# Hybrid decoder layer: order of the down projection's loads, and of splits and small tiles where two stages meet

## The chip, the cores and the metric

The kernel runs on one core of a Trainium2 chip. The metric is the device time in microseconds (us) of one execution, lower is better. Other times below come from one profiled execution, whose own clock starts at zero.

## The reference, cut to what matters

One layer (model width 2048, 512 tokens, all fp32): a token mixer, a cross-attention, a SwiGLU channel mixer and a last norm. The change lies in the channel mixer:

```python
D_FF = -(-8 * D_MODEL // (3 * 256)) * 256        # 5632

def swiglu(h, w_gate_up, w_down):
    gu = h @ w_gate_up
    g, u = gu[..., :D_FF], gu[..., D_FF:]
    return (jax.nn.silu(g) * u) @ w_down

    ...
    h = h + swiglu(rms_norm(h, g_ffn[l]), w_gate_up[l], w_down[l])
return rms_norm(h, g_final)
```

## The kernel before

Every fp32 operand is split into a high part, which ScalarE (ACT) writes by copying into the rounded type, and a low part, the difference, which VectorE (DVE) writes. Each product is then three matmuls: high·high, low·high, high·low. So before TensorE (PE) may use a piece of weights, a load must land, ACT must write the high part (`hi`, L894, or L1181 in the blocks), and DVE the low part (`lo`, L1284, or L1734 in the blocks). Four semaphores carry this: a raw buffer is loaded, high ready, low ready, used.

The hidden width 5632 is 44 tiles of 128. **Tiles 0 to 3** are computed by plain products (line group G_U0 is the last of them). DVE's `first_hidden` (L1725, L1727: two operations a tile) scales and multiplies them out of four banks, ACT's `hidden_hi` (L1151) and DVE's `hidden_lo` (L1708) split each tile, and GpSimd's queue (POOL) spills it to DRAM (L505).

**Tiles 4 to 43** are the 40 blocks. A block computes a gate and an up tile by a Strassen-like scheme of seven products named P1, Q5, P2, P6, P7, P4, P3, each of two halves of 12 matmuls with 256 columns (L835 to L837). `cycle_products` gives the order: P1 and Q5 of block 0 first, then for each block b: P2, P6, P1 of b+1, P7, Q5 of b+1, P4, P3. Some weights are sums of loaded pieces; DVE makes them in place (`sum_x1` to `sum_x4`, L1742 to L1761, 128x1024). The splits go into eight slots, in turn. ACT takes snapshots of a bank between products (`copy_p1` L1190, `copy_p1_p6` L1197, `copy_p1_p6_p7` L1204) and does the silu (L1210); DVE takes the outputs out: `gate_first`, `gate_second` (L1777), `up_second`, `up_first` (L1790), `up_scaled` (L1796), `hidden_out` (L1802).

**The down stage** multiplies all 44 hidden tiles, read back from DRAM, with `w_down`: eight column groups, hh = 0, 1 (hidden tiles 0 to 21 and 22 to 43) by c = 0 to 3 (512 output columns), each of 22 steps k. A step is 12 matmuls with 512 columns (L524 to L526), with k's 128 rows of weights in one of four slots (`w_hi`, `w_lo`). The raw weights come in loads of 256 rows, p = 0 to 10 for a column group, into the four raw buffers; a load may be issued once the low parts of the load four before it are written. The hidden tiles are loaded by `hidden_load(h)` into places in SBUF that the blocks leave: 0 to 11 into `s_res`, each four once a product is done, 12 to 27 into `h_both`, 28 and 29 into `s_res`, all of these 18 once the last block is done. The residual comes back from DRAM in four parts into `acc`, which needs the last spill to have landed, as they share SBUF. Column group c adds onto part c.

What sets the order is written by hand: each engine runs its instructions strictly as written, and a wait holds up all that stands behind it. SyncE's queue (SP) issues all the loads. Before, SP issues the first four raw loads of the down stage (L462), then all 30 hidden tiles (L454), then the four parts of the residual (L468), and then the other raw loads (L381). ACT and DVE finish the last block's silu, up and hidden output and then split the first four steps of weights.

Of the kernel before, what the change touches and what calls it, by code (L numbers as in the profile page):

```python
# [46 lines left out]
HT = FF // P  # L47
HH = HT // 2
# [24 lines left out]
B_DOWN = B_U0 + KT  # L73
# [16 lines left out]
SPL = 4  # L90
# [13 lines left out]

def cycle_products(b):

    more = b + 1 < BLOCKS
    return [("P2", b), ("P6", b)] + [("P1", b + 1)] * more + [("P7", b)] + [("Q5", b + 1)] * more + [("P4", b), ("P3", b)]


def product_counts():
# [14 lines left out]
def build(nc, x, mem, g_mix, w_in, conv_w, sinks, w_attn_o, w_conv_o, w_out, g_xattn, g_mem,  # L126
          w_xq, w_xkv, w_xo, g_ffn, w_gate_up, w_down, g_final, rope, out):
    with ExitStack() as ctx:
# [235 lines left out]
        def _(sp):  # L364
# [91 lines left out]
            def down_load(hh, c, p):  # L456

                load((B_DOWN + HH * (4 * hh + c)) // 2, 0, None, p, wd, hh * HH * P + 256 * p, 512 * c)

            for p in range(RAW):  # L460
                sp.wait_ge(s_blo, NUMBER["P7" if p == 1 else "P3" if p == 3 else "P4", BLOCKS - 2] + 2)
                sp.dma_start(raw[:, p, :, :], wd[256 * p:256 * p + 256, 0:512].rearrange("(b p) n -> p b n", p=P)).then_inc(s_raw[p], 16)  # L462
            for h in range(len(PLACES)):
                hidden_load(h)
            for i in range(2):
                sp.wait_ge(s_hsp[i], 16 * (HT // 2))
            for c in range(4):
                sp.dma_start(acc[:, 4 * c:4 * c + 4, :], acc_dram[c]).then_inc(s_ald[c], 16)  # L468
            for hh in range(2):
                for c in range(4):  # L470
                    for p in range(HH // 2):
                        if hh or c or p >= RAW:
                            down_load(hh, c, p)
                        if hh and c == 0 and 2 * p + len(PLACES) < HT:
                            hidden_load(len(PLACES) + 2 * p)
                            hidden_load(len(PLACES) + 2 * p + 1)
# [403 lines left out]
        def _(act):  # L880
            def hi(b0, g, k, gain=None, per=0, gper=0, i=None):

                n = (b0 + k) // 2
                s = (b0 + k) % SPL
                if k % 2 == 0:
                    act.wait_ge(s_raw[n % RAW], 16 * (n // RAW + 1) + (i * (2 * per) if i is not None else 0))

                if k == SPL - 1 and g:
                    act.wait_ge(s_done, 4 * g + (i * (4 * gper) if i is not None else 0))
                elif b0 + k >= SPL:  # L890
                    before = g if k >= SPL else g - 1
                    act.wait_ge(s_used, b0 + k - SPL + 1 - before + (i * (per - gper) if i is not None else 0))
                sc = 1.0 if gain is None else gain[:, k:k + 1]
                nc.scalar.activation(w_hi[:, s, :], raw[:, n % RAW, (b0 + k) % 2, :], ACT.Copy, scale=sc).then_inc(s_hi, 1)  # L894
# [251 lines left out]
            def hidden_hi(h):  # L1146

                act.wait_ge(s_upp, h + 1)
                if h >= 2:
                    act.wait_ge(s_hsp[h % 2], 16 * (h // 2))  # L1150
                nc.scalar.activation(hid_t[:, h % 2, 0, :], up_t[:, h % 2, :], ACT.Copy).then_inc(s_ahi, 1)  # L1151
# [31 lines left out]
            def copy_p1(b):  # L1183

                act.wait_ge(s_bused, NUMBER["P1", b] + 2)
                if b >= 2:
                    act.wait_ge(s_g1, b - 1)
                elif b == 1:
                    act.wait_ge(s_upp, 4)
                nc.scalar.activation(snap[b % 2][SNAP_A], reg_a[b % 2][:, 0:TH], ACT.Copy).then_inc(s_ca, 1)  # L1190
# [15 lines left out]
            def silu(b):  # L1206

                act.wait_ge(s_g1n, b + 1)
                act.wait_ge(s_g2, b + 1)
                nc.scalar.activation(gate_t[:, b % 2, :], gate_t[:, b % 2, :], ACT.Silu).then_inc(s_silu, 1)  # L1210

            block_hi("P1", 0)
            block_hi("Q5", 0)
            hidden_hi(0)
            hidden_hi(1)
            copy_p1(0)
            for b in range(BLOCKS):
                for name, n in cycle_products(b):
                    block_hi(name, n)
                    if name == "P2" and b == 0:  # L1220
                        hidden_hi(2)
                        hidden_hi(3)
                    if name == "P6" and b:
                        silu(b - 1)
                    if name == "P7":
                        copy_p1_p6(b)
                        if b:
                            hidden_hi(3 + b)
                    if name == "P4":
                        copy_p1_p6_p7(b)  # L1230
                        if b + 1 < BLOCKS:
                            copy_p1(b + 1)
            silu(BLOCKS - 1)
            for k in range(SPL):
                act.wait_ge(s_bused, HALVES - SLOTS + k + 1 if (HALVES + k) % SLOTS < SPL else HALVES)
                hi(B_DOWN, G_DOWN, k)
            hidden_hi(HT - 1)
            for k in range(SPL, HH):
                hi(B_DOWN, G_DOWN, k)
# [18 lines left out]
        def _(dve):  # L1258
# [446 lines left out]
            def hidden_lo(h):  # L1705

                dve.wait_ge(s_ahi, h + 1)
                nc.vector.tensor_tensor(hid_t[:, h % 2, 1, :], up_t[:, h % 2, :], hid_t[:, h % 2, 0, :], ALU.subtract).then_inc(s_alo, 1)  # L1708
# [10 lines left out]
            def first_hidden(j):  # L1719

                done(G_U0, j)
                dve.wait_ge(s_gate, 32 + j + 1)
                if j >= 2:
                    dve.wait_ge(s_alo, j - 1)
                nc.vector.tensor_tensor(up_t[:, j % 2, :], banks(G_U0)[j][:, :], rbc[:, :], ALU.mult).then_inc(s_freed, 1)  # L1725
                dve.wait_ge(s_freed, 4 * G_U0 + j + 1)
                nc.vector.tensor_tensor(up_t[:, j % 2, :], up_t[:, j % 2, :], tile4[:, j, :], ALU.mult).then_inc(s_upp, 1)  # L1727
# [9 lines left out]
            def sum_x1(b):  # L1737

                dve.wait_ge(s_braw[b % 2][1], 16 * (b // 2 + 1))
                dve.wait_ge(s_blo, NUMBER["P1", b] + 2)  # L1740
                w = braw[b % 2]
                nc.vector.tensor_tensor(w[:, 0, :, :], w[:, 0, :, :], w[:, 1, :, :], ALU.add).then_inc(s_x1, 1)  # L1742
# [8 lines left out]
            def sum_x3(b):  # L1751

                dve.wait_ge(s_x1, b + 1)
                w = braw[b % 2]
                nc.vector.tensor_tensor(w[:, 1, :, :], w[:, 1, :, :], w[:, 3, :, :], ALU.add).then_inc(s_x3, 1)
# [36 lines left out]
            def up_scaled(b):  # L1792

                dve.wait_ge(s_u1, b + 1)
                dve.wait_ge(s_u2, b + 1)
                nc.vector.tensor_tensor(up_t[:, b % 2, :], up_t[:, b % 2, :], rbc[:, :], ALU.mult).then_inc(s_un, 1)  # L1796

            def hidden_out(b):

                dve.wait_ge(s_silu, b + 1)  # L1800
                dve.wait_ge(s_un, b + 1)
                nc.vector.tensor_tensor(up_t[:, b % 2, :], up_t[:, b % 2, :], gate_t[:, b % 2, :], ALU.mult).then_inc(s_upp, 1)  # L1802
# [2 lines left out]
            sum_x1(0)  # L1805
            block_lo("Q5", 0)
            sum_x2(0)
            first_hidden(0)
            first_hidden(1)
            hidden_lo(0)  # L1810
            first_hidden(2)
            hidden_lo(1)
            first_hidden(3)
            for b in range(BLOCKS):
                for name, n in cycle_products(b):
                    block_lo(name, n)
                    if name == "P2":
                        sum_x3(b)
                        if b:
                            gate_second(b - 1)  # L1820
                        else:
                            hidden_lo(2)
                            hidden_lo(3)
                    if name == "P6":
                        if b:
                            up_first(b - 1)
                        sum_x4(b)
                        if b:
                            up_scaled(b - 1)
                    if name == "P1":  # L1830
                        if b:
                            hidden_out(b - 1)
                        sum_x1(n)
                    if name == "P7":
                        if b + 1 == BLOCKS:
                            hidden_out(b - 1)
                        gate_first(b)
                        if b:
                            hidden_lo(3 + b)
                    if name == "Q5":  # L1840
                        sum_x2(n)
                    if name == "P4":
                        up_second(b)
            gate_second(BLOCKS - 1)
            up_first(BLOCKS - 1)
            up_scaled(BLOCKS - 1)
            hidden_out(BLOCKS - 1)
            for k in range(SPL):
                lo(B_DOWN, 0, None, k)
            hidden_lo(HT - 1)  # L1850
            for k in range(SPL, HH):
                lo(B_DOWN, 0, None, k)
# [69 lines left out]
```

## Time and profile before

| what | value |
|---|---|
| time, median of 3 runs | 2753.96 us (2753.07 to 2754.15) |
| the profiled execution | 2752.59 us, of which span 2750.8 us |
| PE / DVE / ACT busy | 98% / 58% / 39% of the span |
| mean granted clock of PE | 0.992 |
| PE, longest waits | 20.0 us and 3.0 us (L524), 4.7 us (L835) |

PE is a pipeline: a row's time from start to end is longer than the distance to the next start, so the pace is read from the starts: 0.12 us for 256 columns and 0.227 us for 512 at full clock. At half clock they are 0.21 and 0.43. The profile's rows give the idle time of an engine ahead of a row in square brackets, and who ended it. SPq rows are the issue of loads, not their transfer.

### The profile page before, as it was taken

How to read it: one execution, taken by the hardware profiler on the slowest of the kernel's cores; microseconds unless marked ns; L12 is line 12 of the kernel's file. 1: busy time of each engine (PE TensorE's matmuls, PEld its weight loads, DVE VectorE, ACT ScalarE, POOL GpSimd, SP SyncE). 2: the span in 40 equal slices, each digit the busy share in tenths (PEclk: the TensorE clock that was granted, in tenths of full speed). 3: DMA queues.
4: the chain of work that ended last, by engine and by line, in shares of the span. 5: the costliest groups of instructions: out<-in, count | busy, mean ns of one | idle time of the engine just before them, and what ended most of it. 6: DMA issues, size and time to landing. Idle time of an engine off the chain costs nothing.

```text
span 2750.8 us, 39364 instructions
## 1 busy us (share of the span) xinstructions
PE 2702.6 (98%) x15433; PEld 2385.9 (87%) x15433; DVE 1587.9 (58%) x2791; ACT 1071.5 (39%) x1996; POOL 28.8 (1%) x60
## 2 busy tenths in 40 slices
PE   8999999999999999999999999999999969999998
PEld 7888888888888888887889999999999968888887
DVE  4557775333333445457778888888888833222334
ACT  4334543323232333345644444444444422222221
POOL 0000000000000000000000000000000000000000
PEclk9999999999999999999999999999999989999999
DMA  5332222333333333333444434444344493235232
GB/s 165 96 92 77 77 75 87 100 93 98 99 92 99 97 111 113 95 114 121 138 138 126 143 116 139 131 131 139 116 144 126 123 369 113 94 121 183 93 99 92
DMA packets 277058, 328.40 MB, mean 119 GB/s; under 512 B 10444, under 2 KB 174372, under 8 KB 274980
## 3 DMA queue, kind: packets, MB, share of 16 engines
q1 hardware_dynamic: 269572, 295.82, 35.2%
q0 software_dynamic: 7328, 30.41, 2.7%
q8 instruction: 106, 1.74, 0.3%
q14 instruction: 52, 0.43, 0.0%
HBM read 294.74 MB, written 31.46 MB: 119 GB/s over the span
## 4 chain that ended last, share of the span: by engine, by line
PE 95%; DVE 2%; SPq 1%; DMA 1%; issue 0%; ACT 0%; DVEq 0%
PE bank L524 19%; PE bank L525 19%; PE bank L526 19%; PE bank L835 10%; PE bank L837 10%; PE bank L836 10%; PE bank L539 2%; PE bank L541 2%; PE bank L540 2%; SPq L454 1%; DMA raw<-in_w_down_dram 1%; PE bank L646 1%; PE bank L632 0%; DVE y_out L1897 0%; DVE h_lo L1309 0%
## 5 line engine op out<-in xcount | busy, mean ns | idle before, releaser
L1284 DVE TENSOR_TENSOR w_lo<-raw,w_hi 128x512 fp32r<-128x512 f32 x352 | 243.2, 692 | 564.8 <-ACT w_hi L894 563.8
L894 ACT ACTIVATE w_hi<-raw 128x512 fp32r<-128x512 f32 x352 | 221.8, 631 | 647.8 <-PE bank L526 616.8
L1286 DVE SCALAR_TENSOR_TENSOR w_lo<-raw,par,w_hi 128x512 fp32r<-128x512 f32 x320 | 239.9, 751 | 394.6 <-ACT w_hi L894 393.7
L524 PE MATMUL bank<-h_hi,w_hi 128*128 128x512 f32 x1088 | 428.0, 393 | 0.0
L526 PE MATMUL bank<-h_hi,w_lo 128*128 128x512 f32 x1088 | 423.8, 390 | 0.0
L525 PE MATMUL bank<-h_lo,w_hi 128*128 128x512 f32 x1088 | 423.8, 390 | 0.0
L894 ACT ACTIVATE w_hi<-raw,par 128x512 fp32r<-128x512 f32 x320 | 231.3, 724 | 467.0 <-PE bank L526 380.8
L526 PEld LDWEIGHTS bank<-h_hi,w_lo 128*128 128x128 f32 x1088 | 204.2, 188 | 43.5
L524 PEld LDWEIGHTS bank<-h_hi,w_hi 128*128 128x128 f32 x1088 | 204.4, 188 | 40.3 <-issue 0.2
L525 PEld LDWEIGHTS bank<-h_lo,w_hi 128*128 128x128 f32 x1088 | 204.5, 188 | 40.0
L1734 DVE TENSOR_TENSOR w_lo<-braw,w_hi 128x512 fp32r<-128x512 f32 x280 | 179.7, 686 | 13.8 <-ACT w_hi L1181 13.8
L524 PE MATMUL bank<-s_res,w_hi 128*128 128x512 f32 x416 | 163.6, 393 | 23.0 <-DVE w_lo L1284 23.0
L835 PE MATMUL bank<-s_hi,w_hi 128*128 128x256 f32 x648 | 183.5, 283 | 0.5 <-ACT snap L1197 0.5
L1734 DVE TENSOR_TENSOR h_lo<-braw,h_hi 128x512 fp32r<-128x512 f32 x280 | 179.5, 686 | 7.5 <-ACT h_hi L1181 7.4
L836 PE MATMUL bank<-s_lo,w_hi 128*128 128x256 f32 x648 | 183.4, 283 | 0.0
L837 PE MATMUL bank<-s_hi,w_lo 128*128 128x256 f32 x648 | 183.4, 283 | 0.0
L835 PE MATMUL bank<-s_hi,h_hi 128*128 128x256 f32 x632 | 178.9, 283 | 0.0
L836 PE MATMUL bank<-s_lo,h_hi 128*128 128x256 f32 x632 | 178.8, 283 | 0.0
L837 PE MATMUL bank<-s_hi,h_lo 128*128 128x256 f32 x632 | 178.8, 283 | 0.0
L525 PE MATMUL bank<-s_res,w_hi 128*128 128x512 f32 x416 | 163.1, 392 | 0.0
L526 PE MATMUL bank<-s_res,w_lo 128*128 128x512 f32 x416 | 163.0, 392 | 0.0
L1181 ACT ACTIVATE w_hi<-braw 128x512 fp32r<-128x512 f32 x280 | 158.3, 624 | 11.5 <-PE bank L526 6.2
(259 smaller groups left out, 5989.0 us busy)
## 6 DMA issues: line engine op xcount, KB each, us to landing
braw<-in_w_gate_up_dram SPq DMA_DIRECT2D x160, 512.0 KB, 4.7
raw<-in_w_in_dram SPq DMA_DIRECT2D x136, 512.0 KB, 3.7
raw<-in_w_down_dram SPq DMA_DIRECT2D x88, 512.0 KB, 3.7
hidden_spilled<-hid_t POOLq DMA_DIRECT2D x44, 512.0 KB, 3.6
raw<-in_w_out_dram SPq DMA_DIRECT2D x32, 512.0 KB, 3.6
s_res<-hidden_spilled SPq DMA_DIRECT2D x26, 512.0 KB, 7.5
h_both<-hidden_spilled SPq DMA_DIRECT2D x18, 512.0 KB, 11.6
raw<-in_w_conv_o_dram SPq DMA_DIRECT2D x16, 512.0 KB, 3.7
```

The lines of the kernel that those rows point to most:

```text
L524: pe.matmul(o_, w_hi[:, s, c], hi, start=(k == 0), stop=False)
L525: pe.matmul(o_, w_hi[:, s, c], lo, start=False, stop=False)
L526: mm = pe.matmul(o_, w_lo[:, s, c], hi, start=False, stop=(k == n - 1))
L539: pe.matmul(bk[j][:, :], hi[:, c], w_hi[:, s, :], start=(k == 0), stop=False)
L835: pe.matmul(r[:, 0:TH], w_h[:, q, :], u_h, start=(not on and half == 0 and q == 0), stop=False, skip_group_check=on)
L836: pe.matmul(r[:, 0:TH], w_h[:, q, :], u_l, start=False, stop=False, skip_group_check=on)
L837: mm = pe.matmul(r[:, 0:TH], w_l[:, q, :], u_h, start=False, stop=(half == 1 and q == 3), skip_group_check=on)
L894: nc.scalar.activation(w_hi[:, s, :], raw[:, n % RAW, (b0 + k) % 2, :], ACT.Copy, scale=sc).then_inc(s_hi, 1)
L1181: nc.scalar.activation(slot_hi[n % SLOTS], weights(name, b)[:, 4 * half:4 * half + 4, :], ACT.Copy).then_inc(s_bhi, 1)
L1284: nc.vector.tensor_tensor(w_lo[:, s, :], src, w_hi[:, s, :], ALU.subtract).then_inc(s_lo, 1)
L1286: nc.vector.scalar_tensor_tensor(w_lo[:, s, :], src, g[:, k:k + 1], w_hi[:, s, :], ALU.mult, ALU.subtract).then_inc(s_lo, 1)
L1734: nc.vector.tensor_tensor(slot_lo[n % SLOTS], weights(name, b)[:, 4 * half:4 * half + 4, :], slot_hi[n % SLOTS], ALU.subtract).then_inc(s_ ...
```

## The change

`cycle_products` is written in another way with the same result. The rest is order.

```diff
@@ SP, the down stage @@
-            for h in range(len(PLACES)):
+            for h in range(12):
                 hidden_load(h)
-            for i in range(2):
-                sp.wait_ge(s_hsp[i], 16 * (HT // 2))
-            for c in range(4):
-                sp.dma_start(acc[:, 4 * c:4 * c + 4, :], acc_dram[c]).then_inc(s_ald[c], 16)
             for hh in range(2):
                 for c in range(4):
                     for p in range(HH // 2):
+                        if hh == 0 and c == 0 and 4 <= p < 9:
+                            hidden_load(2 * p + 4)
+                            hidden_load(2 * p + 5)
                         if hh or c or p >= RAW:
                             down_load(hh, c, p)
+                        if hh == 0 and 1 <= c < 3 and p < 4:
+                            hidden_load(HH + 4 * (c - 1) + p)
+                        if hh == 0 and p == 9:
+                            if c == 0:
+                                for i in range(2):
+                                    sp.wait_ge(s_hsp[i], 16 * (HT // 2))
+                            sp.dma_start(acc[:, 4 * c:4 * c + 4, :], acc_dram[c]).then_inc(s_ald[c], 16)
@@ ACT @@
             block_hi("P1", 0)
             block_hi("Q5", 0)
-            hidden_hi(0)
-            hidden_hi(1)
-            copy_p1(0)
             for b in range(BLOCKS):
                 for name, n in cycle_products(b):
                     block_hi(name, n)
                     if name == "P2" and b == 0:
-                        hidden_hi(2)
-                        hidden_hi(3)
-                    if name == "P6" and b:
-                        silu(b - 1)
+                        copy_p1(0)
+                    if name == "P6":
+                        if b:
+                            silu(b - 1)
+                        else:
+                            hidden_hi(0)
+                            hidden_hi(1)
                     if name == "P7":
                         copy_p1_p6(b)
-                        if b:
-                            hidden_hi(3 + b)
+                        hidden_hi(3 + b if b else 2)
+                    if name == "Q5" and b == 0:
+                        hidden_hi(3)
...
+            for k in range(SPL):
+                act.wait_ge(s_bused, HALVES - SLOTS + k + 1)
+                hi(B_DOWN, G_DOWN, k)
             silu(BLOCKS - 1)
-            for k in range(SPL):
-                act.wait_ge(s_bused, HALVES - SLOTS + k + 1 if (HALVES + k) % SLOTS < SPL else HALVES)
-                hi(B_DOWN, G_DOWN, k)
             hidden_hi(HT - 1)
@@ DVE @@
             sum_x2(0)
-            first_hidden(0)
-            first_hidden(1)
-            hidden_lo(0)
-            first_hidden(2)
-            hidden_lo(1)
-            first_hidden(3)
...
+            for k in range(SPL):
+                lo(B_DOWN, 0, None, k)
             gate_second(BLOCKS - 1)
             up_first(BLOCKS - 1)
             up_scaled(BLOCKS - 1)
             hidden_out(BLOCKS - 1)
-            for k in range(SPL):
-                lo(B_DOWN, 0, None, k)
             hidden_lo(HT - 1)
```

Inside DVE's loop over the blocks, `first_hidden` and `hidden_lo` of tiles 0 to 3 now stand among the first products: behind P2's splits and `sum_x3` tiles 0 and 1; behind P6's and `sum_x4` the low part of tile 0, tile 2, the low part of tile 1; behind P1's tile 3; behind Q5's the low part of tile 2; and in block 1, behind P2's, the low part of tile 3.

**First place: DVE, between the weight sums of block 0.** Names: `braw0` and `braw1` hold raw weights of even and odd blocks, `h_lo` and `w_lo` as outputs are low parts of a half product, `up_t` with `bank` and then with `tile4` are the two operations of `first_hidden`, `hid_t` is `hidden_lo`. Before:

```order
1220 L1749 TENSOR_TENSOR braw0_93<-braw0_93 128x1024
1221 L1725 TENSOR_TENSOR up_t_96<-bank0,rbc_103 128x512
1222 L1727 TENSOR_TENSOR up_t_96<-up_t_96,tile4_100 128x512
...
1229 L1725 TENSOR_TENSOR up_t_96<-bank3,rbc_103 128x512
1230 L1727 TENSOR_TENSOR up_t_96<-up_t_96,tile4_100 128x512
1231 L1734 TENSOR_TENSOR h_lo_50<-braw0_93,h_hi_49 128x4x128 x2
1232 L1755 TENSOR_TENSOR braw0_93<-braw0_93 128x1024
1233 L1708 TENSOR_TENSOR hid_t_97<-up_t_96,hid_t_97 128x512 x2
1234 L1734 TENSOR_TENSOR h_lo_50<-braw0_93,h_hi_49 128x4x128 x2
```

The four tiles and two low parts stood ahead of P2's low parts. In the changed kernel, the same engine and place:

```order
1220 L1757 TENSOR_TENSOR braw0_93<-braw0_93 128x1024
1221 L1742 TENSOR_TENSOR h_lo_50<-braw0_93,h_hi_49 128x4x128 x2
1222 L1763 TENSOR_TENSOR braw0_93<-braw0_93 128x1024
1223 L1733 TENSOR_TENSOR up_t_96<-bank0,rbc_103 128x512
...
1227 L1742 TENSOR_TENSOR h_lo_50<-braw0_93,h_hi_49 128x4x128 x2
1228 L1769 TENSOR_TENSOR braw0_93<-braw0_93 128x1024
1229 L1716 TENSOR_TENSOR hid_t_97<-up_t_96,hid_t_97 128x512
1230 L1733 TENSOR_TENSOR up_t_96<-bank2,rbc_103 128x512
...
1233 L1742 TENSOR_TENSOR w_lo_53<-braw1_94,w_hi_52 128x512 x2
1234 L1733 TENSOR_TENSOR up_t_96<-bank3,rbc_103 128x512
```

P2's two low parts now come right behind the sum, and the tiles are spread behind the splits of P2, P6 and P1.

**Second place: DVE, from the last block to the down stage.** `w_lo` out of `raw` is a low part of down weights. Before:

```order
1983 L1777 TENSOR_TENSOR gate_t_95<-bank7,rbc_103 128x256
1984 L1790 TENSOR_TENSOR up_t_96<-bank0,snap1_102 128x256
1985 L1796 TENSOR_TENSOR up_t_96<-up_t_96,rbc_103 128x512
1986 L1802 TENSOR_TENSOR up_t_96<-up_t_96,gate_t_95 128x512
1987 L1284 TENSOR_TENSOR w_lo_53<-raw_51,w_hi_52 128x512 x4
1988 L1708 TENSOR_TENSOR hid_t_97<-up_t_96,hid_t_97 128x512
```

The four low parts closed the row. In the changed kernel they stand ahead of the gate's second half:

```order
1984 L1292 TENSOR_TENSOR w_lo_53<-raw_51,w_hi_52 128x512 x4
1985 L1785 TENSOR_TENSOR gate_t_95<-bank7,rbc_103 128x256
1986 L1798 TENSOR_TENSOR up_t_96<-bank0,snap1_102 128x256
1987 L1804 TENSOR_TENSOR up_t_96<-up_t_96,rbc_103 128x512
1988 L1810 TENSOR_TENSOR up_t_96<-up_t_96,gate_t_95 128x512
1989 L1716 TENSOR_TENSOR hid_t_97<-up_t_96,hid_t_97 128x512
```

ACT's four high parts move in the same way, ahead of the last silu.

**Third place: SP, from the last block into the down stage.** Before:

```order
178 L454 DMA s_res<-hidden_spilled 128x1024 x12
179 L454 DMA h_both<-hidden_spilled 128x2x512 x16
180 L454 DMA s_res<-hidden_spilled 128x1024 x2
181 L468 DMA acc<-residual_spilled 128x2048 x4
182 L381 DMA raw<-in_w_down_dram 128x2x512 x41
```

In the changed kernel:

```order
178 L455 DMA s_res<-hidden_spilled 128x1024 x12
179 L455 DMA h_both<-hidden_spilled 128x2x512 x2
180 L382 DMA raw<-in_w_down_dram 128x2x512
181 L455 DMA h_both<-hidden_spilled 128x2x512 x2
182 L382 DMA raw<-in_w_down_dram 128x2x512
183 L455 DMA h_both<-hidden_spilled 128x2x512 x2
184 L382 DMA raw<-in_w_down_dram 128x2x512
...
188 L382 DMA raw<-in_w_down_dram 128x2x512 x2
189 L480 DMA acc<-residual_spilled 128x2048
190 L382 DMA raw<-in_w_down_dram 128x2x512 x2
191 L455 DMA h_both<-hidden_spilled 128x2x512
```

Eighteen hidden tiles and four parts of the residual stood ahead of the fifth raw load; now two hidden tiles do, and the rest goes between later raw loads.

## Rows read from the trace of the kernel before

**Rows 1.** Page, busy time by engine (first line), and PE's waits: total, times, longest.
```profile
PE 2702.6 (98%) x15433; PEld 2385.9 (87%) x15433; DVE 1587.9 (58%) x2791; ACT 1071.5 (39%) x1996; POOL 28.8 (1%) x60
...
PE bank L524 <- DVE w_lo L1284: 23.0, 2, 20.0
PE bank L835 <- DVE h_lo L1734: 4.7, 1, 4.7
```

**Rows 2.** Timeline of PE around the long wait: start, us, engine, line, operation, count, [idle].
```profile
2250.60 0.39 PE L526 MATMUL bank<-s_res,w_lo 128*128 128x512 f32 x1
2271.00 0.79 PE L524 MATMUL bank<-s_res,w_hi 128*128 128x512 f32 x1 [20.01 <-DVE w_lo L1284]
...
2275.00 0.43 PE L524 MATMUL bank<-s_res,w_hi 128*128 128x512 f32 x1
```

**Rows 3.** Timeline of SP's queue and of ACT, from the last block into the down stage.
```profile
2203.03 17.44 SPq L454 DMA_DIRECT2D s_res<-hidden_spilled  x12
2224.51 20.98 SPq L454 DMA_DIRECT2D h_both<-hidden_spilled  x16
...
2247.44 3.11 SPq L468 DMA_DIRECT2D acc<-residual_spilled  x4
2250.60 46.14 SPq L381 DMA_DIRECT2D raw<-in_w_down_dram  x10
...
2269.59 1.15 ACT L894 ACTIVATE w_hi<-raw 128x512 fp32r<-128x512 f32 x2 [28.81 <-DMA raw<-in_w_down_dram]
```

**Rows 4.** Raw loads of line L381, 2200 to 2300 us: issue to landing.
```profile
DMA to landing us min/median/max: 3.6/4.4/19.7
```

**Rows 5.** Stretches: length, busy PE, PEld, DVE, ACT, POOL, clock granted, DMA share, GB/s.
```profile
2214.00:2218.00 4.00, 3.52 (x28) 3.11 (x26) 1.90 (x3) 1.95 (x4) 0.53 (x1) 1.00 0.66 223
2226.00:2228.00 2.00, 0.57 (x2) 0.51 (x3) 2.00 (x4) 0.63 (x1) 0.00 (x0) 0.82 1.02 420
2228.00:2230.00 2.00, 2.00 (x6) 1.62 (x5) 1.47 (x3) 0.00 (x0) 0.23 (x1) 0.50 1.02 398
2240.00:2250.00 10.00, 10.00 (x46) 8.29 (x45) 0.69 (x1) 0.63 (x1) 0.00 (x0) 1.00 1.05 387
```

**Rows 6.** Timeline of PE where the blocks end and the down stage begins.
```profile
2224.20 0.28 PE L837 MATMUL bank<-s_hi,h_lo 128*128 128x256 f32 x1
2227.43 0.77 PE L524 MATMUL bank<-s_res,w_hi 128*128 128x512 f32 x1 [2.95 <-DVE w_lo L1284]
...
2230.86 0.39 PE L526 MATMUL bank<-s_res,w_lo 128*128 128x512 f32 x1
```

**Rows 7.** Timeline of DVE and ACT there.
```profile
2224.51 0.42 DVE L1790 TENSOR_TENSOR up_t<-bank,snap 128x256 f32<-128x256 f32 x1 [2.45 <-PE bank L837]
2226.38 2.49 DVE L1284 TENSOR_TENSOR w_lo<-raw,w_hi 128x512 fp32r<-128x512 f32 x4
...
2218.31 1.14 ACT L1181 ACTIVATE h_hi<-braw 128x512 fp32r<-128x512 f32 x2
2222.70 2.17 ACT L894 ACTIVATE w_hi<-raw 128x512 fp32r<-128x512 f32 x4
```

**Rows 8.** Timeline of PE at the first block.
```profile
1409.24 0.28 PE L835 MATMUL bank<-h_hi,w_hi 128*128 128x256 f32 x1
...
1419.84 0.55 PE L835 MATMUL bank<-h_hi 128*128 128x256 f32 x1 [4.68 <-DVE h_lo L1734]
...
1425.10 0.31 PE L835 MATMUL bank<-s_hi,h_hi 128*128 128x256 f32 x1
```

**Rows 9.** Timeline of DVE at the first block.
```profile
1410.90 1.22 DVE L1749 TENSOR_TENSOR braw<-braw 128x1024 f32<-128x1024 f32 x1
1412.04 0.68 DVE L1725 TENSOR_TENSOR up_t<-bank,rbc 128x512 f32<-128x512 f32 x1
...
1413.37 0.68 DVE L1725 TENSOR_TENSOR up_t<-bank,rbc 128x512 f32<-128x512 f32 x1
...
1419.01 1.28 DVE L1734 TENSOR_TENSOR h_lo<-braw,h_hi 128x512 fp32r<-128x512 f32 x2
1420.21 1.22 DVE L1755 TENSOR_TENSOR braw<-braw 128x1024 f32<-128x1024 f32 x1
...
1434.36 0.42 DVE L1783 TENSOR_TENSOR up_t<-bank,mask 128x256 f32<-128x256 f32 x1 [0.99 <-ACT mask L1204]
```

More of the change, by code:

```diff
@@ L105, in cycle_products @@
 def cycle_products(b):
-    more = b + 1 < BLOCKS
-    return [("P2", b), ("P6", b)] + [("P1", b + 1)] * more + [("P7", b)] + [("Q5", b + 1)] * more + [("P4", b), ("P3", b)]
+    if b + 1 == BLOCKS:
+        return [("P2", b), ("P6", b), ("P7", b), ("P4", b), ("P3", b)]
+    return [("P2", b), ("P6", b), ("P1", b + 1), ("P7", b), ("Q5", b + 1), ("P4", b), ("P3", b)]
 def product_counts():
@@ L1818, in _ @@
                         sum_x3(b)
+                        if b == 0:
+                            first_hidden(0)
+                            first_hidden(1)
+                        elif b == 1:
+                            hidden_lo(3)
                         if b:
                             gate_second(b - 1)
-                        else:
-                            hidden_lo(2)
-                            hidden_lo(3)
                     if name == "P6":
@@ L1829, in _ @@
                             up_scaled(b - 1)
+                        else:
+                            hidden_lo(0)
+                            first_hidden(2)
+                            hidden_lo(1)
                     if name == "P1":
@@ L1832, in _ @@
                             hidden_out(b - 1)
+                        else:
+                            first_hidden(3)
                         sum_x1(n)
@@ L1841, in _ @@
                         sum_x2(n)
+                        if b == 0:
+                            hidden_lo(2)
                     if name == "P4":
                         up_second(b)
+            for k in range(SPL):
+                lo(B_DOWN, 0, None, k)
             gate_second(BLOCKS - 1)
```

## The prediction

> **What bounds the kernel now.** I read the busy times first: PE is busy for 2702.6 of 2750.8 us [rows 1], so only its idle time and its slow stretches can be won. The list of PE's waits comes next: three waits hold 27.7 us of the 48.2 us of idle time, 20.0 and 3.0 us for low parts of down weights and 4.7 us for a low part in the first block [rows 1]. Then the timeline around each, because after each of them PE also runs at half clock (1.2 instead of 2.4 GHz) for a while: the granted clock falls while PE waits (0.82 in 2226 to 2228 us) and is 0.50 behind it [rows 5]. So a wait costs its idle time and the slow matmuls behind it.
>
> **Part 1, the order of loads.** PE's last matmul ahead of the long wait starts at 2250.60 and takes 0.227 us, so it is through at 2250.83; the next starts at 2271.00: 20.17 us idle. The 9 matmuls from there to 2275.00, where the pace is normal again, take 4.00 us instead of 9 x 0.227 = 2.04: 1.96 us [rows 2]. Together 22.1 us. ACT shows who is late: its high part at 2269.59 had waited 28.81 us for a raw load. SP issued that load at 2250.60, behind the rest of the hidden tiles (2224.51) and the residual (2247.44) [rows 3], and it took 19.7 us to land where the median is 4.4 [rows 4]: the bytes queued ahead of it had to go first. Its buffer was free long before: the low parts that it waits for were written by 2228 us [rows 7].
>
> In the changed order the fifth raw load has only hidden tiles 12 and 13 ahead of it. When does it land? With many in flight, 387 GB/s move [rows 5], so a load of 524 KB takes 1.35 us. The last hidden tiles of `s_res` were issued by 2220.5 (2203.03 + 17.44) [rows 3]. At most four of them are then under way, 5.4 us, so the queue is empty at 2225.9 at the latest. Three loads more: 2230.0. The spill of the last tile and the final gain on GpSimd's queue (1.5 MB) share the engines, 4.1 us at most: 2234. When is it needed? Steps 0 to 7 of the first column group have their weights; with PE starting at 2225.1 (next part) and 12 x 0.227 = 2.72 us a step, step 8 starts at 2246.9, its splits must begin 1.4 us earlier: 2245.5. The margin is 15.5 us, or 11.5 with GpSimd's traffic. Each later raw load is issued when the low parts four loads back are written, that is one every 5.44 us, with two hidden tiles before it: three loads, 4.06 us of transfer, in 5.44. The margin grows. Hidden tile 12 is needed at 2225.1 + 12 x 2.72 = 2257.7 and is issued at 2224.5; tile 20 at 2279.5, issued behind the seventh raw load at about 2237. In column groups 1 and 2 one hidden tile goes beside each of four raw loads (2.7 us in 5.44). The first part of the residual is issued when the low parts of steps 10 and 11 are written, about 2225.1 + 8 x 2.72 + 1.4 = 2248, and is needed when the column group ends at 2285; its wait for the last spill, with seven raw loads already in or ahead, was over by about 2236. What is late next in this stage: nothing that I find. I count the whole 22.1 us.
>
> The Trainium skill, DMA: Bandwidth & Descriptors, "Queues, rings and completion order", says that completion is not first in, first out for one issuing engine. By that the raw load would not be sure to pass what is issued after it: with all eight loads that SP can issue by then sharing the engines, and GpSimd's traffic, it would land at 2225.9 + 10.8 + 4.1 = 2240.8, a margin of 4.7 us instead of 11.5, and the sum would stay. It is why I leave a chance for a short rest of this wait. This case's trace looks like order of issue: 18 hidden tiles (24.3 us), the residual (10.8), GpSimd's traffic (4.1) and the load itself (1.4) on top of 2225.9 give 2266.5, and ACT had it at 2269.6 [rows 3].
>
> **Part 2, the splits ahead of the last block's output.** PE's last block matmul starts at 2224.20 and is through at 2224.32; the first of the down stage starts at 2227.43: 3.11 us. The 8 matmuls to 2230.86 take 3.43 us instead of 1.81: 1.62 us [rows 6]. Together 4.7 us. The wait was for low parts at 2226.38 [rows 7]. In the new order ACT's four high parts start behind P3's splits (2218.31 + 1.1 = 2219.4) and end by 2221.6; the four slots were left by P6 and P7 before that. DVE's low parts end near 2222.3. Then the next wait in PE's program decides: the first two column groups wait until `up_first` has read its bank, and that cannot start before the last P3 is done, 2224.51, plus 0.42 [rows 7]. PE then starts at about 2225.1: 0.8 us stay. Does the clock stay up? Around a wait of 0.47 us it was 1.00 [rows 5]; around 2.95 us it fell. 0.8 is near the first. Gain 4.7 - 0.8 = 3.9 us; 2.3 us if the clock falls still; 4.2 if only 0.5 us stay. The silu and tile 43 are covered: that tile is read in the last half.
>
> **Part 3, the first block.** P1 and Q5 take 48 matmuls at 0.12 us from 1409.24 and end at 1415.0; P2 starts at 1419.84, 4.84 us later, and its 24 matmuls last until 1425.10, 5.26 instead of 2.88 [rows 8]. Together 7.2 us. But DVE is without idle time here from 1410.90 to 1434 us [rows 9], so the work put off must be done among the next products. Its pace from rows 9: a sum 1.14 us (1410.90 to 1412.04), a `first_hidden` 1.33 (1412.04 to 1413.37), a pair of low parts 1.20 (1419.01 to 1420.21), a `hidden_lo` half of that, 0.60; a result is there 0.7 us after its start. I go through the new order from 1412.04. P2's pair 1412.04, the sum, tiles 0 and 1 (2.66): P6's pair at 1417.04, its first half ready at 1417.7, and PE wants it at 1415.0 + 2.88 = 1417.9: no wait. Then sum, `hidden_lo`, tile 2, `hidden_lo`, with 0.14 for a dependence: 1.14 + 0.60 + 1.33 + 0.60 + 0.14 later P1's pair starts, at 1422.05; ready for PE at 1422.9, wanted at 1420.8: **2.1 us of new wait**. Tile 3 and a sum: P7's pair at 1425.7, ready at 1426.5, wanted at 1422.9 + 2.88 = 1425.8: **0.8 us**. The gate's first half (0.8): Q5's pair at 1427.7, wanted 1429.4; a sum and `hidden_lo`: P4's pair at 1430.7, wanted 1432.3. DVE has caught up. So PE reaches P4 at 1415.0 + 5 x 2.88 + 2.9 = 1432.3, where before it did at 1425.10 + 4 x 2.88 = 1436.6: 4.3 us, of the 7.2. ACT is not late: its work for P2 moves ahead of two short splits. Bounds: nothing new (7.2), and the slow clock again for one product behind the 2.1 us (4.3 - 2.4 = 1.9). A wait of 2.1 us lies between the 0.47 that kept the clock and the 2.95 that did not, and is nearer to the latter, but PE works up to it and behind it; I take 4.3.
>
> **Sum.** 22.1 + 3.9 + 4.3 = 30.3 us. The profiled execution's span would be 2750.8 - 30.3 = 2720.5. The profiled execution took 2752.59, 1.4 under the median; I take the difference from the median: 2753.96 - 30.3 = 2723.7.
>
> **Rivals.** (a) The clock falls at a wait that is left, in the first block or at the entry (or both): 22.1 + 2.3 + 1.9 = 26.3 us at the least, 2727.7. For it: it fell at 2.95 us; against it: each of the new waits is shorter. (b) A rest of the long wait stays, because raw loads do not pass the hidden tiles: a wait of some 4.4 us (one landing) with its slow clock, 1.96: 30.3 - 6.4 = 23.9, 2730.1. Against it: the margins above. (c) Slower than before: with a queue that is fed in step with the splits, transfers might run one after the other at their full latency, 4.4 us each [rows 4], instead of 1.35. Then three take 13.2 us in each 5.44 us; the raw load p (4 to 8) lands at 2225.9 + 13.2 x (p - 3), and p = 8, needed at 2267.3, is there at 2291.9: 24.6 late. Column groups 1 and 2 add four times 8.8 - 5.44 each, 26.9, and regain 7 x 1.04 between them. That is 44 us lost where 30.3 were saved: 2768. It decides from 4.0 us for each. Against it: 387 GB/s with several in flight, and they are issued together. (d) The first block wins all 7.2: 33.2 us, 2720.8; the DVE sum speaks against it. (e) The change does not do what it says: some other wait in front of SP's raw load keeps the 20 us, and only 8.2 us are won: 2745.8. I find no such wait.
>
> **Chances.** Forecast 0.76 (its own 2721.5 to 2726), (a) 0.11, (b) 0.05, (c) 0.03, (d) 0.03, (e) 0.02. The range reaches from (d) to a little beyond (a), 2720.5 to 2729. About 0.2% (5.5 us) is what a measurement of this kernel can tell from no change. All but (c) are faster by more: 0.97. Of (c), 0.02 is slower, and 0.01 is latencies so near its deciding point that nothing shows.
>
> **What would show it.** Right: no wait of PE above 1 us between 2225 and 2700 us, a first down matmul some 0.8 us behind the last block matmul with clock 1.00, the fifth raw load landing in about 5 to 10 us; in the first block two waits of about 2.1 and 0.8 us, for `w_lo` of P1 and of P7, instead of one of 4.7. Wrong: a wait of ACT for a raw load in the first column group (part 1), one of PE for a hidden tile (part 1), a wait for `w_lo` at the entry (part 2), a granted clock of 0.50 in the 10 us behind any of them, or waits that come back in block 1 and later because DVE has not caught up (part 3).

## The result

The changed kernel takes 2723.0 us (median, 2722.67 to 2723.27) against 2753.7 us of the kernel before on the same chip: the ratio is 0.9889, with a 95% interval of 0.9871 to 0.9906. That is 30.7 us; the prediction had 30.3 and 2723.7. The interval of the ratio allows 25.9 to 35.5 us. The profiled execution has a span of 2720.9 us, where the sum gave 2720.5.

The busy times and PE's list of waits, which answer to [rows 1] (waits: total us, times, longest). Line numbers are 1 to 12 higher than before.

```profile
PE 2696.8 (99%) x15433; PEld 2381.3 (88%) x15433; DVE 1587.4 (58%) x2791; ACT 1072.1 (39%) x1996; POOL 28.8 (1%) x60
...
PE bank L546 <- DVE w_lo L1294: 3.1, 1, 3.1
PE bank L842 <- DVE w_lo L1742: 2.7, 2, 2.1
PE bank L531 <- issue: 0.6, 1, 0.6
```

The waits of 20.0, 3.0 and 4.7 us are gone. In place of the last are two of 2.1 and 0.6 us for low parts, and 0.6 us of "issue" is left at the entry to the down stage. (The 3.1 us are the kernel's first matmul of weights, which the change doesn't touch.)

PE's and SP's timelines at the entry, for [rows 6] and [rows 3]:

```profile
2220.37 0.28 PE L844 MATMUL bank<-s_hi,h_lo 128*128 128x256 f32 x1
2221.22 0.47 PE L531 MATMUL bank<-s_res,w_hi 128*128 128x512 f32 x1 [0.56 <-issue]
2221.52 0.39 PE L532 MATMUL bank<-s_res,w_hi 128*128 128x512 f32 x1
...
2220.68 1.27 SPq L455 DMA_DIRECT2D h_both<-hidden_spilled  x2
2222.00 0.60 SPq L382 DMA_DIRECT2D raw<-in_w_down_dram  x1
2222.71 1.48 SPq L455 DMA_DIRECT2D h_both<-hidden_spilled  x2
2224.24 0.59 SPq L382 DMA_DIRECT2D raw<-in_w_down_dram  x1
```

The last block matmul is through at 2220.49 and the first down matmul starts at 2221.22, then the pace is 0.23 us at once: the clock stayed up. The fifth raw load is issued 1.3 us behind the first hidden tiles of this batch, where it was 26 us. The stretches behind it, for [rows 5] (length, busy PE, PEld, DVE, ACT, POOL, granted clock, DMA share, GB/s):

```profile
2222.00:2226.00 4.00, 4.00 (x19) 3.33 (x18) 2.02 (x3) 1.26 (x2) 1.06 (x2) 1.00 1.03 412
2226.00:2300.00 74.00, 74.00 (x329) 61.25 (x328) 21.09 (x31) 17.06 (x27) 0.00 (x0) 1.00 0.66 234
```

PE is busy for the whole of the 78 us in which it used to stand for 20. The raw loads of this stretch, from issue to landing, for [rows 4]:

```profile
DMA to landing us min/median/max: 3.5/5.0/14.2
```

And the first block, PE and DVE, for [rows 8, 9]:

```profile
1409.47 0.28 PE L842 MATMUL bank<-h_hi,w_hi 128*128 128x256 f32 x1
...
1423.32 0.36 PE L842 MATMUL bank<-h_hi,w_hi 128*128 128x256 f32 x1 [2.11 <-DVE w_lo L1742]
1426.98 0.36 PE L842 MATMUL bank<-s_hi,w_hi 128*128 128x256 f32 x1 [0.56 <-DVE w_lo L1742]
...
1417.27 1.29 DVE L1742 TENSOR_TENSOR h_lo<-braw,h_hi 128x512 fp32r<-128x512 f32 x2
1422.49 1.29 DVE L1742 TENSOR_TENSOR w_lo<-braw,w_hi 128x512 fp32r<-128x512 f32 x2
1426.15 1.28 DVE L1742 TENSOR_TENSOR w_lo<-braw,w_hi 128x512 fp32r<-128x512 f32 x2
```

The three DVE rows are the pairs of P6, P1 and P7. Shifted by the 0.23 us by which this execution starts the stretch later, the prediction had them at 1417.27, 1422.28 and 1425.9.

**Where the 29.9 us between the two spans came from.** PE's last block matmul starts 3.83 us earlier (2224.20 against 2220.37): the first block, less those 0.23 us. The entry costs 0.7 us of idle time and no slow clock, where it cost 4.7: 3.9 or 4.0. The long wait and its slow clock, 22.1, are gone whole. 3.8 + 3.9 + 22.1 = 29.8.

### The profile page after: what moved, and what is told of

Read it like the earlier page. It is cut to its first block, busy times and chain, and to the rows that moved or that the text cites. A ratio compares the mean times of both kernels' runs of the same rounds, so it can differ in the third digit from the quotient of the medians.

```text
span 2720.9 us, 39364 instructions
## 1 busy us (share of the span) xinstructions
PE 2696.8 (99%) x15433; PEld 2381.3 (88%) x15433; DVE 1587.4 (58%) x2791; ACT 1072.1 (39%) x1996; POOL 28.8 (1%) x60
## 4 chain that ended last, share of the span: by engine, by line
PE 97%; DVE 2%; issue 0%; ACT 0%; DMA 0%; DVEq 0%
PE bank L531 20%; PE bank L533 20%; PE bank L532 20%; PE bank L842 10%; PE bank L844 10%; PE bank L843 10%; PE bank L546 2%; PE bank L548 2%; PE bank L547 2%; PE bank L653 1%; PE bank L639 0%; DVE y_out L1909 0%; DVE h_lo L1317 0%; PE bank L769 0%; PE bank L741 0%
```

## The experiments

My theory was three separate gains. For each there was a rival: loads that do not pass one another, an entry that is worth nothing, a DVE backlog that only moves. Eight kernels tell these apart. All ratios are against the kernel before on the same chip: e1_loads, e2_entry, e3_first and e4_hidden_ahead ran on one chip (2753.5 us), the others on a second (2753.6 us).

| run | what it is | us | ratio (95%) | PE's waits at the three places |
|---|---|---|---|---|
| e1_loads | before + order of loads | 2729.3 | 0.9910 (0.9893 to 0.9927) | 4.7; 3.0; none |
| e2_entry | before + splits at the entry | 2753.5 | 1.0001 (0.9991 to 1.0010) | 4.7; 0.6; 24.4 |
| e3_first | before + order in the first block | 2750.1 | 0.9987 (0.9977 to 0.9997) | 2.1 and 0.6; 3.0; 20.0 |
| e7_after | the changed kernel | 2723.4 | 0.9888 (0.9872 to 0.9905) | 2.1 and 0.6; 0.6; none |
| e8_loads_first | changed, without the entry's part | 2726.3 | 0.9901 (0.9884 to 0.9917) | 2.1 and 0.6; 2.9; none |
| e4_hidden_ahead | changed, all hidden tiles ahead | 2741.3 | 0.9953 (0.9936 to 0.9970) | 2.1 and 0.6; 0.6; 13.9 |
| e9_acc_ahead | changed, residual ahead | 2730.0 | 0.9915 (0.9898 to 0.9932) | 2.1 and 0.6; 0.6; 3.6 |
| e5_spread | changed, DVE's work spread further | 2720.9 | 0.9880 (0.9864 to 0.9897) | 0.2 and 0.2; 0.6; none |

### One part at a time

**e1_loads** takes SP's part of the diff alone.

> The kernel before with the new order of loads alone. My theory: the 20.2 us wait in the down stage and its 1.96 us of slow clock go, nothing else moves: 22.1 us saved, ratio 0.9920; PE still waits 3 us at the entry and 4.7 us at the first block. Rival (loads do not pass one another): a rest of the wait of some 4 us stays, 16 us saved.

It saved 24.2 us, and no wait of the long kind is left. It is 2 us more than expected, which the interval doesn't settle: it allows 20.1 to 29.5 us, and the expected 22.1 lies inside. The profile shows what could have added to it. At the entry PE waits 3 us as before, but the clock did not fall. First the waiting matmul and the next two, then the stretch:

```profile
2228.67 0.47 PE L530 MATMUL bank<-s_res,w_hi 128*128 128x512 f32 x1 [2.98 <-DVE w_lo L1290]
2228.98 0.40 PE L531 MATMUL bank<-s_res,w_hi 128*128 128x512 f32 x1
2229.21 0.39 PE L532 MATMUL bank<-s_res,w_lo 128*128 128x512 f32 x1
...
2228.00:2232.00 4.00, 3.33 (x15) 2.79 (x16) 2.68 (x5) 0.58 (x2) 0.73 (x2) 1.00 1.03 406
```

In the kernel before, behind a wait of the same length, the pace was 0.43 us and the granted clock 0.50 [rows 5, 6]. That is worth 1.6 us. Behind its 4.7 us wait in the first block, e1's slow stretch was 12 matmuls instead of 24, which is 1.2 us. Both were read from one execution.

**e2_entry** takes the splits at the entry alone:

```diff
+            for k in range(SPL):
+                act.wait_ge(s_bused, HALVES - SLOTS + k + 1)
+                hi(B_DOWN, G_DOWN, k)
             silu(BLOCKS - 1)
-            for k in range(SPL):
-                act.wait_ge(s_bused, HALVES - SLOTS + k + 1 if (HALVES + k) % SLOTS < SPL else HALVES)
-                hi(B_DOWN, G_DOWN, k)
```

and DVE's four low parts in the same way.

> The kernel before with the down splits ahead of the last block's output alone. Additive theory, as in my sum: 3.9 us saved, ratio 0.9986. Rival, which I now hold likelier: the fifth raw load lands at a time that SP's queue sets, not PE; PE starts the down stage 2.3 us earlier and then waits longer (about 24 us instead of 20): within 0.5 us of before.

It gave nothing, as the rival said. PE, ACT and SP there:

```profile
2225.06 0.47 PE L524 MATMUL bank<-s_res,w_hi 128*128 128x512 f32 x1 [0.56 <-issue]
2271.53 0.79 PE L524 MATMUL bank<-s_res,w_hi 128*128 128x512 f32 x1 [24.45 <-DVE w_lo L1284]
...
2270.12 1.15 ACT L894 ACTIVATE w_hi<-raw 128x512 fp32r<-128x512 f32 x2 [33.25 <-DMA raw<-in_w_down_dram]
...
2251.05 22.78 SPq L381 DMA_DIRECT2D raw<-in_w_down_dram  x6
```

PE starts the down stage 2.4 us earlier than before (2225.06 against 2227.43), does its eight steps at full clock, and then waits 24.4 us instead of 20.0. The load that it waits for is issued at 2251.05 whatever PE did (2250.60 before). The 4 us won at the entry were swallowed whole.

**e8_loads_first** is the changed kernel without this part, and so asks what it is worth once the long wait is gone.

> The changed kernel without the moved splits at the entry to the down stage. The moved splits alone gave nothing; here the long wait is gone, so their whole worth should show: 2.4 us of idle time (3.0 against 0.6), and 1.6 more in the executions in which the clock falls at the 3 us wait: 2.4 to 4.0 us slower than the changed kernel. If the entry does not matter here either: 0.

2726.3 against 2723.4 us of the changed kernel beside it: 3.0 us, inside the expected 2.4 to 4.0 (the runs don't overlap: 2725.74 to 2727.25 and 2722.65 to 2724.52). So the same edit is worth 0 on the kernel before and 3 us behind the new order of loads.

**e3_first** takes the first block's part alone.

> The kernel before with the new order in the first blocks alone. Theory: everything behind, SP's loads included, moves with PE: 4.1 to 4.3 us saved, ratio 0.9985, with PE waits of 2.1 and 0.6 us for w_lo in place of 4.7. Rival: as with the entry, the loads of the down stage swallow it, 0 us; against it, those loads are themselves released by the blocks' products.

It saved 3.4 us by the medians, with the very waits of the changed kernel; the interval, 0.8 to 6.3 us, leaves the size open, but not the sign, and the rival's 0 is outside. It is less than the expected 4.1 to 4.3, which the interval allows too. The loads of the down stage do not swallow this gain: they are released by the blocks' products and move with them (the long wait stayed at 20.0 us). The parts add up: e8_loads_first holds the parts of e1 and e3 and gained 27.3 us, where these two alone gained 24.2 + 3.4 = 27.6.

### What the order of loads does

**e4_hidden_ahead** is the changed kernel with the tiles as before and only the residual late:

```diff
-            for h in range(12):
+            for h in range(len(PLACES)):
                 hidden_load(h)
...
-                        if hh == 0 and c == 0 and 4 <= p < 9:
-                            hidden_load(2 * p + 4)
-                            hidden_load(2 * p + 5)
...
-                        if hh == 0 and 1 <= c < 3 and p < 4:
-                            hidden_load(HH + 4 * (c - 1) + p)
```

> The changed kernel, but with all 30 hidden tiles ahead of the fifth raw load; the residual's parts stay late. If transfers land in order of issue: 16 more tiles at 1.3 us, the load lands about 21 us later than the 2234 us of the changed kernel, near 2255, and PE waits 12 to 14 us plus 2 us of slow clock: 14 to 16 us slower than the changed kernel, about 15 us faster than before. If the residual's 4 MB was what mattered: no wait. If transfers in flight share the engines and the order matters little: a wait under 5 us.

SP's, PE's and ACT's rows:

```profile
2222.22 20.88 SPq L455 DMA_DIRECT2D h_both<-hidden_spilled  x16
2243.19 2.02 SPq L455 DMA_DIRECT2D s_res<-hidden_spilled  x2
2245.26 14.39 SPq L382 DMA_DIRECT2D raw<-in_w_down_dram  x5
...
2258.71 0.80 PE L526 MATMUL bank<-s_res,w_hi 128*128 128x512 f32 x1 [13.93 <-DVE w_lo L1287]
...
2257.30 1.15 ACT L896 ACTIVATE w_hi<-raw 128x512 fp32r<-128x512 f32 x2 [22.73 <-DMA raw<-in_w_down_dram]
```

The load is there at 2257.3, that is 35.1 us behind the issue of the first `h_both` tile; in the changed kernel it is 13.3 us (2234.0 - 2220.7). The 16 tiles more cost 21.8 us, 1.36 us each, which is 385 GB/s, close to the 387 of [rows 5]. Most of it is spent before the issue: a full queue holds SP up (20.88 us for 16 tiles), so the load is issued 23 us later than in the changed kernel and then takes 12.0 us in both. That delay alone would fit a queue whose transfers share the engines too; the order is shown by the landings. In the changed kernel the load issued at 2222.00 lands at 2234.0, and the transfers that SP issued behind it, in their order, at 2235.7, 2237.1, 2238.4, 2239.8 and 2241.1: none passed another. GpSimd's two transfers, on a queue of their own, landed in between (2231.2 and 2235.4). PE waited 13.9 us, as expected for that case, and both rivals (no wait; under 5 us) are out. In time it is 17.9 us slower than the changed kernel (e7_after, on the other chip), 2 to 4 more than expected, and 12.2 us faster than before where about 15 were expected. 12 slow matmuls (2.6 us) bring the wait to 16.5, and the last 1.4 us I can't place.

The Trainium skill, DMA: Bandwidth & Descriptors, "Queues, rings and completion order", warns that completion is not first in, first out; its example is a transfer on one DMA engine behind one on sixteen. For when a load of this size lands, the trace shows order of issue (1.36 us a tile), so its time can be reckoned from the bytes ahead, here among transfers of 512 KB and 1 MB; that a completion may be relied on without its semaphore is not shown by this, and no run here tried it.

**e9_acc_ahead** puts the residual's four parts, with their wait for the last spill, ahead of the fifth raw load, the tiles staying as in the changed kernel.

> The changed kernel, but with the four parts of the residual (4 MB), and their wait for the last spill, ahead of the fifth raw load. In order of issue: the spill is awaited until about 12 us after the blocks' end, then 10.8 us of residual and 1.4 us of the load itself: it lands some 25 us after the blocks' end where the splits want it at 21: a wait of 3 to 7 us with its slow clock, 3 to 9 us slower than the changed kernel. If the tiles alone made the wait: 0.

```profile
2221.03 1.28 SPq L455 DMA_DIRECT2D h_both<-hidden_spilled  x2
2230.41 3.10 SPq L476 DMA_DIRECT2D acc<-residual_spilled  x4
2233.57 0.43 SPq L382 DMA_DIRECT2D raw<-in_w_down_dram  x1
...
2245.77 1.15 ACT L901 ACTIVATE w_hi<-raw 128x512 fp32r<-128x512 f32 x2 [12.39 <-DMA raw<-in_w_down_dram]
...
2247.18 0.79 PE L531 MATMUL bank<-s_res,w_hi 128*128 128x512 f32 x1 [3.59 <-DVE w_lo L1292]
```

The load lands 24.7 us behind the first tile's issue (25 expected), PE waits 3.6 us and runs at half clock behind it, and the kernel is 6.6 us slower than the changed one (3 to 9 expected). SP stands from 2222.3 to 2230.4 for the spill, with nothing issued. So tiles and residual both had to leave the way; either alone in front leaves a wait.

### DVE's backlog in the first block

**e5_spread** is the changed kernel with DVE's work of block 0 put by need. The sum for P4 and the two sums for block 1 come later, tiles 2 and 3 too:

```diff
                     if name == "P6":
...
                         else:
                             hidden_lo(0)
-                            first_hidden(2)
-                            hidden_lo(1)
                     if name == "P1":
...
                         else:
-                            first_hidden(3)
-                        sum_x1(n)
+                            first_hidden(2)
                     if name == "P7":
+                        if b == 0:
+                            sum_x1(1)
+                            hidden_lo(1)
                     if name == "Q5":
+                            sum_x4(0)
                     if name == "P4":
+                            gate_first(0)
+                            hidden_lo(2)
+                            sum_x2(1)
                         up_second(b)
+                    if name == "P3" and b == 0:
+                        first_hidden(3)
```

The low part of tile 3 stands one product later, behind P6's splits of block 1. ACT's `hidden_hi` of tiles 2 and 3 follow, and its first snapshot of block 1 waits for two tiles out instead of four, as it overwrites only what tiles 0 and 1 read.

> The changed kernel with DVE's small work of the first blocks spread further: the weight sums wait until just ahead of their use, tile 2 comes behind P1's splits, tile 3 behind P3's, and its low part in block 1. My going through the DVE order from the measured paces gives waits of about 0.2 and 0.5 us in place of 2.1 and 0.6: 2.0 us saved, 2721. If it is not DVE's load but some latency that makes the 2.1 us wait, the wait stays and nothing is saved. If DVE's backlog is only pushed into block 1, waits of about 2 us in all come up there.

PE's waits from 1405 to 1450 us, then the stretch from 1410 to 1450 of the kernel before, of the changed kernel and of this one:

```profile
PE bank L842 <- DVE h_lo L1745: 0.2, 1, 0.2
PE bank L842 <- DVE w_lo L1745: 0.2, 1, 0.2
```
```profile
1410.00:1450.00 40.00, 35.31 (x275) 35.14 (x275) 35.54 (x53) 17.73 (x36) 2.13 (x4) 0.91 0.33 108
```
```profile
1410.00:1450.00 40.00, 37.33 (x309) 36.97 (x309) 38.78 (x58) 19.32 (x38) 2.66 (x5) 1.00 0.43 136
```
```profile
1410.00:1450.00 40.00, 39.63 (x324) 39.11 (x323) 36.97 (x56) 20.49 (x41) 2.66 (x5) 1.00 0.42 134
```

The second and third numbers are the stretch and PE's busy time: 35.3, 37.3, 39.6 us of 40, at a clock of 0.91, 1.00, 1.00. The kernel takes 2720.9 us against 2723.4 of the changed kernel beside it, 2.4 us less (their fastest and slowest runs don't overlap: 2720.17 to 2721.57 and 2722.65 to 2724.52). The backlog was DVE's order of work, not a latency, and it did not come back in block 1. This version beats both kernels: 0.9880 of the time before.

## Why the prediction was right

**The bound.** PE's idle time and the slow clock behind it were all that the change could win, and were what it won. PE's busy time fell by 5.8 us (2702.6 to 2696.8), and the slow matmuls behind the three waits had cost 6.0 (2.4, 1.6 and 2.0); the other 24 us were idle time. That the sum met the medians within 0.4 us is in part luck: the interval is far wider, and two executions of one kernel differ by 1 to 2 us.

**Part 1, loads.** The 22.1 us came whole, and the reason held: e4 and e9 put back what was ahead and the wait came back as the queue's bytes give it. One step was mis-sized, and not on the safe side: it took 3.8 us of the margin, which was wide enough. I had the fifth raw load land at 2230.0, or 2234 with GpSimd's traffic, in the time of the kernel before; that is 2226.2 and 2230.2 in the changed one. It landed at 2234.0, 12.0 us after its issue, and the two behind it took 14.2 us. The margin to 2241.7, the last moment at which its splits could begin without holding PE up, was 7.7 us, not 11.5 to 15.5. What I had wrong is "at most four of them are then under way". The last `s_res` tile, in the kernel before (first line) and in the changed one (second):

```profile
DMA to landing us min/median/max: 9.9/9.9/9.9
DMA to landing us min/median/max: 10.3/10.3/10.3
```

It was issued at 2219.96 and landed at 2229.9, where I had the queue empty by 2225.9. Six of these tiles and a spill of GpSimd's (issued at 2216.34) landed behind 2220.5, seven times 1.35 us and not four. In the changed kernel it landed at 2226.3 instead of 2222.1, and the fifth raw load is late by nearly the same. With a full queue a raw load took 12 us in e4 and e9 too; the median of 4.4 us [rows 4] is that of loads with little or nothing ahead of them.

**Part 2, entry.** 3.9 us were predicted and came, by the mechanism told: PE's first down matmul starts at 2221.22, 0.1 us behind the end of `up_first`:

```profile
2220.69 0.42 DVE L1798 TENSOR_TENSOR up_t<-bank,snap 128x256 f32<-128x256 f32 x1 [1.51 <-PE bank L844]
```

What the sum did not say is that this term hangs on part 1. It was written as a separate gain, and e2 shows that alone it is worth nothing, since a load that lands at its own time ends the next wait. In the sum it did no harm, because part 1 stood ahead of it. The size holds only where the clock would have fallen: e8 measures 3.0 us.

**Part 3, first block.** 7.2 us less 2.9 of new waits; measured 2.11 and 0.56 us of new waits, and P4 starts 4.0 us earlier, counted from P1, against 4.3 predicted. Going through DVE's new order with measured paces gave the starts of the pairs of P6, P1, P7 and Q5 within 0.25 us and that of P4 within 0.4.

**The clock.** It stayed up at all the waits that are left, as I took it. That it falls at a 3 us wait was read from one execution and is not a property of the wait, as e1 shows.

**The rivals.** (a) did not occur in the profiles of the changed kernel; (b) and (c), a rest of the wait and serial transfers, are against e4's 1.36 us a tile; (d) falls with the 2.1 us; (e) with the vanished wait.

## What to carry to other kernels

Put the transfers of one queue in the order of their use, and reckon what stands ahead of a load in bytes: here 1.36 us for each half megabyte, in order of issue, plus what other queues move at that time. Before adding up the gains of several edits, ask for each whether the next wait is ended by something that the edit moves too: an earlier start in front of a wait for a load whose issue doesn't move is worth nothing until that wait is gone. Where small work is moved off the path of one engine, add up that engine's work between the next deadlines; e5 found 2.4 us more by moving what was not yet needed.

## What I had not expected of the hardware

The slow clock behind a wait is not fixed by the wait. Behind waits of 2.98 us (e1) and 2.95 us (before, e8) the clock stayed at 1.00 in the first and fell to 0.50 in the others, while at the 2.1 us wait it stayed at 1.00 in every profile that has one; and behind the same 4.7 us wait 24 matmuls were slow in one execution and 12 in another. The kernel's start varies in the same way: P1 of block 0 starts at 1409.2 us in one profile and 1411.5 in another of kernels that are alike up to there. Below are the first matmul of weights and the stretch around it, each in two profiles.

```profile
18.50 0.52 PE L539 MATMUL bank<-w_hi,h_hi 128*128 128x512 f32 x1 [2.87 <-DVE w_lo L1286]
```
```profile
19.38 0.80 PE L546 MATMUL bank<-w_hi,h_hi 128*128 128x512 f32 x1 [3.55 <-DVE w_lo L1294]
```
```profile
17.00:24.00 7.00, 5.50 (x17) 4.43 (x18) 3.47 (x7) 2.64 (x6) 0.00 (x0) 0.76 0.71 203
```
```profile
17.00:24.00 7.00, 4.62 (x11) 3.66 (x12) 4.31 (x7) 2.36 (x4) 0.00 (x0) 0.60 0.56 162
```

The first and third are of the kernel before, the others of e7, whose span is 1.8 us longer than that of the changed kernel's first profile although the kernel is the same (though perhaps on another chip). So differences of 1 to 2 us between single profiles say nothing here, and a gain of that size has to be read from the waits.
